# First loads of a decoder step spread over two DMA queues, and its last result row stored in halves

## The reference, cut to what matters

```python
h = rmsnorm(x, g_mix_pre)
proj = h @ w_in                      # q, k, v, the conv branch's B, C, u and two gates
...
x = x + rmsnorm(merged @ w_o, g_mix_post)
h2 = rmsnorm(x, g_ffn_pre)
...
x = x + rmsnorm(f, g_ffn_post)
x = x + jax.nn.sigmoid(x @ w_ple_gate) * (p @ w_ple)
```

## Time and profile before

| what | us |
|---|---|
| median of three runs | 2642.64 (2642.46 to 2642.98) |
| profiled execution, first to last instruction | 2641.4 |
| PE busy in it | 2631.3 |
| DVE, ACT, POOL busy | 2263.1, 1413.3, 194.9 |

### The profile page before, as it was taken

How to read it: one execution, slowest core, us unless ns; L and a number is a source line. 1 busy time by engine, 2 the same in 40 slices (tenths; PEclk the granted TensorE clock), 3 DMA queues, 4 the chain that set the end, 5 groups by cost and what they waited for, 6 DMA issues and landing times.

```text
span 2641.4 us, 55478 instructions
## 1 busy us (share of the span) xinstructions
PE 2631.3 (100%) x20853; PEld 2571.7 (97%) x20853; DVE 2263.1 (86%) x4000; ACT 1413.3 (54%) x2592; POOL 194.9 (7%) x296
## 2 busy tenths in 40 slices
PE   9999999999999999999999999999999999999999
PEld 8999999999999999999999999999999999999899
DVE  7988888888899987898888888888888768789987
ACT  6544555555566555655555555555555463445444
POOL 0221000000011000000000000000000000000000
PEclk9999999999999999999999999999999999999999
DMA  6666334333487555756566655665569575565774
GB/s 229 186 202 182 133 127 139 133 126 119 157 291 225 165 171 151 266 152 181 166 189 190 189 156 168 187 208 166 157 195 310 150 247 169 161 206 165 246 262 155
DMA packets 162481, 487.12 MB, mean 184 GB/s; under 512 B 17337, under 2 KB 51521, under 8 KB 158928
## 3 DMA queue, kind: packets, MB, share of 16 engines
q1 hardware_dynamic: 129184, 372.41, 39.9%
q0 software_dynamic: 32976, 112.38, 18.9%
q10 hardware_dynamic: 144, 0.15, 0.0%
HBM read 426.42 MB, written 57.30 MB: 183 GB/s over the span
## 4 chain that ended last, share of the span: by engine, by line
PE 65%; DVE 1%; issue 0%; ACT 0%; DVEq 0%; ACTq 0%
PE pair L1221 56%; PE pair L1186 5%; PE pair L1124 2%; PE pair L1298 1%; PE pair L1320 1%; DVE v_lo L1979 0%; DVE lo L2353 0%; PE pair L1081 0%; DVE v_lo L1976 0%; ACT o_hi L1455 0%; DVE s_raw L2278 0%; DVE s_raw L2297 0%; ACT v_hi L1390 0%; DVE lo_A L2353 0%; PE pair L1275 0%
## 5 line engine op out<-in xcount | busy, mean ns | idle before, releaser
L1221 PE MATMUL pair<-o_hi,v_hi 128*128 128x260 f32 x5840 | 1656.2, 284 | 1.9 <-DVE v_lo L1979 1.4
L1221 PE MATMUL pair<-o_hi,v_lo 128*128 128x260 f32 x5840 | 1648.9, 282 | 0.0
L1390 ACT ACTIVATE v_hi<-s_raw 128x512 fp32r<-128x512 f32 (+1 forms) x1384 | 861.7, 626 | 884.8 <-PE pair L1221 795.4
L1221 PE MATMUL pair<-lo,v_hi 128*128 128x260 f32 x4172 | 1178.5, 282 | 0.0
L1979 DVE TENSOR_TENSOR v_lo<-s_raw,v_hi 128x512 fp32r<-128x512 f32 (+1 forms) x1288 | 873.2, 680 | 296.1 <-ACT v_hi L1390 261.5
L1221 PEld LDWEIGHTS pair<-o_hi,v_hi 128*128 128x128 f32 x5840 | 1098.0, 188 | 15.6 <-issue 12.5
L1221 PEld LDWEIGHTS pair<-o_hi,v_lo 128*128 128x128 f32 x5840 | 1099.9, 188 | 0.0
L1221 PEld LDWEIGHTS pair<-lo,v_hi 128*128 128x128 f32 x4172 | 784.1, 188 | 0.2
L1390 ACT ACTIVATE v_hi<-s_one 128x512 fp32r<-128x512 f32 (+1 forms) x228 | 142.2, 626 | 192.6 <-PE pair L1221 164.2
L1221 PE MATMUL pair<-lo_E,v_hi 128*128 128x260 f32 x834 | 236.0, 283 | 0.0
L1221 PE MATMUL pair<-lo_A,v_hi 128*128 128x260 f32 x834 | 235.2, 282 | 0.0
(11 more groups left out here) (301 smaller groups left out, 2595.4 us busy)
## 6 DMA issues: line engine op xcount, KB each, us to landing
s_raw<-in_sstream SPq DMA_DIRECT2D x468, 512.0 KB, 4.9
s_one<-in_sstream POOLq DMA_DIRECT2D x168, 512.0 KB, 5.2
raw<-f_scr SPq DMA_DIRECT2D x12, 1040.0 KB, 7.7
s_raw<-in_sstream SPq DMA_DIRECT2D x32, 384.0 KB, 4.1
g_scr<-d_h SPq DMA_DIRECT2D x16, 520.0 KB, 2.7
g_in<-g_scr SPq DMA_DIRECT2D x32, 260.0 KB, 4.0
x_scr<-y_sb SPq DMA_DIRECT2D x8, 1040.0 KB, 5.3
s_one<-in_sstream POOLq DMA_DIRECT2D x32, 256.0 KB, 4.6
```

The lines of the kernel that those rows point to most:

```text
L1221: mm = pe.matmul(out, wt[:, slot, kk * P:kk * P + P], r[:, k, :], start=j in (0, 1, 3) and k == 0 and n == 0, stop=k == nk - 1 and n == 2, ...
L1390: nc.scalar.activation(v_hi[:, n % 4, 0:width], src, ACT.Copy, scale=0.5 if halved(u) else 1.0).then_inc(v_hi_rdy, 1)
```

## The change

The weight pieces of parts 0 to 2 (rows 0 to 3) leave SP's queue and go to ACT's. There they are cut otherwise: the pieces of row 0 alone count on `kv_first`, those of rows 1 to 3 on a new `kv_second`, for which PE waits ahead of row 1. The constants are split: the 16 columns of gains go first on ACT's queue (`gain_ready`), the other 280 last of its six loads; three of the six stand behind ACT's first table load and activation. ACT waits for `x_part[2]` at 16, since no weights count on it any more, and for the rest of `chan` just ahead of its first use. At the end, the upper half of row 15 is stored by itself as soon as DVE has added it (`half_out`), then row 14, then the lower half of row 15. The arithmetic is the same.

```diff
             for i, (a, b) in enumerate(X_PARTS):
                 sp.dma_start(x_raw[:, a:b, :], x_in[:, a:b, :]).then_inc(x_part[i], 16)
                 for q in (a // KH, 2 + a // KH):
-                    if i == 0:
-                        kv_piece(q, 0, 2, kv_first)
-                    elif i > 1:
+                    if i > 2:
                         kv_piece(q, a, b, s_rdy[0][q] if b % KH == 0 else x_part[i])
...
+            def last_store():
+                i = 7
+                row = d_sb[i % 2]
+                sp.wait_ge(half_out, 1)
+                sp.dma_start(y_out[2 * i + 1, :, HALF:T], row[:, 1, HALF:T]).then_inc(y_stored[i % 2], 16)
+                sp.wait_ge(x_out, 2 * i + 1)
+                sp.dma_start(y_out[2 * i, :, :], row[:, 0, :]).then_inc(y_stored[i % 2], 16)
+                sp.wait_ge(x_out, 2 * i + 2)
+                sp.dma_start(y_out[2 * i + 1, :, 0:HALF], row[:, 1, 0:HALF]).then_inc(y_stored[i % 2], 16)
...
-                gate_store(i)
+                if i < 7:
+                    gate_store(i)
+                else:
+                    last_store()
...
             for i in range(2):
-                sp.wait_ge(y_stored[i], 16 * KD // 2)
+                sp.wait_ge(y_stored[i], 16 * (KD // 2 + i))
...
                     if k == 0:
                         pe.wait_ge(kv_first, 32)
+                    if k == 1:
+                        pe.wait_ge(kv_second, 32)
...
-            act.dma_start(chan[:, :], chan_in).then_inc(chan_ready, 16)
+            act.dma_start(chan[:, 0:KD], chan_in[:, 0:KD]).then_inc(gain_ready, 16)
+            for q in (0, 2):
+                act.dma_start(s_raw[0][q][:, 0:P], sstream[0, q, :, 0:P]).then_inc(kv_first, 16)
             act.wait_ge(pool_set, 1)
             nc.scalar.activation(table_out[:, 6:7], ones[:, 0:1], ACT.Sqrt)
+            for q in (0, 2):
+                act.dma_start(s_raw[0][q][:, P:4 * P], sstream[0, q, :, P:4 * P]).then_inc(kv_second, 16)
+            act.dma_start(chan[:, KD:NCHAN], chan_in[:, KD:NCHAN]).then_inc(chan_ready, 16)
...
-            act.wait_ge(chan_ready, 16)
+            act.wait_ge(gain_ready, 16)
             for i, (a, b) in enumerate(X_PARTS):
-                act.wait_ge(x_part[i], 16 if i < 2 or b % KH == 0 else 48)
+                act.wait_ge(x_part[i], 16 if i < 3 or b % KH == 0 else 48)
...
+            act.wait_ge(chan_ready, 16)
             bias = chan[:, C_BGATE:C_BGATE + 2 * KD]
...
-                st.done(last_half(HALF, T, 2 * i + 1))
+                last_half(HALF, T, 2 * i + 1).then_inc(half_out, 1)
```

More of the change, by code:

```diff
@@ L512, in build @@
         kv_first = sem("kv_first")
+        kv_second = sem("kv_second")
+        gain_ready = sem("gain_ready")
+        half_out = sem("half_out")
         bias_half = sem("bias_half")
```

## The result

| | before | with the change |
|---|---|---|
| median of 21 runs, us | 2642.64 (2641.84 to 2644.26) | 2646.06 (2644.32 to 2648.00) |
| profiled span, us | 2641.4 | 2646.1 |
| PE busy in it, us | 2631.3 | 2631.9 |

The ratio is 1.0014, with a 95% interval of 1.0008 to 1.0019: slower by 3.4 us, where 0.6 us of gain was forecast and 2643.4 us was the upper end of the range. It is within 0.2%, as forecast, but the sign is wrong.

A forecast was written before the change was run, and what follows sets the result against it. PE was taken to bound the kernel, busy 2631.3 of 2641.4 us. Gains of 0.1 (row 0), 0.2 (row 2) and 0.3 us (end) sum to 0.6 us, from 2642.64 to 2642.0 us; range 2641.2 to 2643.4.

The forecast's parts named there:

- Start, what is added: ACT's six issues where it had one: weights for row 1 land at 7.5 us, no PE wait, 0.2 us of cover.
- a queue that is emptier: Argument that the 192 KB pieces for rows 1 to 3 on ACT's queue land at 7.1 to 8.1 us.
- Start, rows 2 and 3: x's rows 2 and 3 issued third, no weights counted: row 2 scaled by 7.8 us, PE's 0.20 us gap goes.
- a column takes twice as long at the start: PE's warm-up pace at the start: time won there may count for half, 0.06 to 0.12 us, taken as 0.1.
- the second weight pieces become the wait: Rival at row 1: pieces issued after ACT's activation land at 8.6 to 9.6 us; 2643.4 us, chance 0.15.
- The rival of issues that hold each other up: At the start, ACT's and SP's issues take twice 0.44 us, row 0 comes 1.5 us late; 2643.5 us, chance 0.05.
- a sign of being wrong: Issues of ACT or SP of 0.8 us in the first 4 us would show the prediction wrong.
- ACT's scaling of row 0: At the start, ACT's first scaling would come near 4.2 us, where it came at 4.54 us.
- the constants' rest costs nothing: The rest of the constants, issued at 2.9 us, is first used after PE's sum at 31.06 us: no cost.
- as the prediction assumed of a gain: The 0.3 us gained at the start carries through PE's sum at 31.06 us to the end.
- The end's 0.3 us: Last store of 130 KB in place of 260 KB lands 0.3 us sooner, bounds 0.1 and 0.5 us.
- the gain of 0.3 us at the start: PE's gaps ahead of rows 0 and 2 go, worth 0.1 and 0.2 us.

The follow-up runs named there:

- e3: The changed kernel, but SP holds back x's rows 2 and 3, and all behind them, until row 0's weights have landed; 2641.79 us.
- e1: The changed kernel with the new start alone; the end stores whole rows as before; 2646.11 us.
- e5: The changed kernel with 24 warm-up matmul pairs on PE in place of 9; 2644.62 us.
- e11: The changed kernel with 20 warm-up matmul pairs on PE in place of 9; 2644.64 us.
- e2: The kernel before with the new end alone, the last row stored in halves; 2641.72 us.
- e7: The changed kernel, but weights of rows 0 and 1 stay on SP's queue; only those of rows 2 and 3 go to ACT's; 2643.28 us.
- e4: The changed kernel, but SP loads x's rows 2 to 5 one at a time, in packets half as long; 2644.68 us.
- e8: The changed kernel, but ACT's first two weight pieces hold rows 0 to 3 at once and the second pair is gone; 2647.06 us.
- e10: The changed kernel, but SP waits until x's row 0 has landed before it issues x's rows 2 and 3; 2643.03 us.

## Why the prediction was wrong

*The step that failed* is "Start, what is added". It had the gains and row 0's two pieces "issued by 0.73 + 3 x 0.44 = 2.05 us", which is right (2.11), and left row 0 there: the landing of these two pieces, for which PE waits first of all, got no term in the sum and no rival. The argument given for the pieces of rows 1 to 3, that "a queue that is emptier" serves them sooner, was the wrong picture for both pairs. The old second piece took 3.5 us from issue on SP's queue, and I carried that over in effect. It took 6.7 us, because a place in one queue is no place in the other, and the change put the two-row load of x beside it at the same moment. e3 shows it by taking that load, and all behind it, away for the time of the wait: 3.3 us to landing, no gap on PE, and 4.3 us less in all.

*"Start, rows 2 and 3"* took it as safe to move x's load up from fifth to third place: "even at the old landing time" ACT would be in time. It was, in its way: row 2 was scaled from 8.14 us, earlier than 9.14 before. The load's own landing was checked; whom it pushes aside was not. Issued 1 us earlier, it landed 1 us later than before (8.1 against 7.1) and held up the weights.

*Pace had no term.* The prediction noted that a column takes twice as long at the start and used it to halve a gain. That a late row 0 could bring the lower pace back, as in the profiled change, or meet a clock that has not risen yet (e1, first entry at 13.9 us), was not weighed. In the profiled run of the change it cost 1.89 us more than before, and e5 confirms it from the other side: without the stop 24.81 us for the same instructions.

*The rival that came nearest* was "the second weight pieces become the wait". It named the pieces of rows 1 to 3 and their issue behind the activation. ACT's queue did not wait for the activation (2.20 us, not 3.5), and yet the pieces landed at 9.2 and 11.0 us, the second later than the rival's 8.6 to 9.6. PE did not wait for them, only because row 0 was later still; in e11, where row 0 came at 7.81 us, it did, for 0.68 us.

*The rival of issues that hold each other up* fell: ACT's issues took 0.40 to 0.67 us and SP's first four 1.81 / 4 = 0.45 us, side by side. SP's issue of x's rows 6 and 7, at 3.61 us, did take 1.19 us, which the prediction named as a sign of being wrong, but every load for which PE stood had been issued by then. No run shows the doubled 0.44 us from which 2643.5 us was worked out. The second issuing engine brought the issues forward, and not the landing: SP's first four loads are issued by 2.55 us, and the third lands with ACT's third at 8.1 to 8.4 us.

*What held.* ACT's scaling of row 0 moved from 4.54 to 3.88 us, and the constants' rest costs nothing. What PE's sum loses reaches the end undiminished, 4.8 us at the sum and 4.7 at the end, as the prediction assumed of a gain. The end's 0.3 us is borne out as a size in most profiles, not in the change's own: from DVE's last addition to the span's end it was 2.6 us in the two profiles with the old end (before, e1), and of the twelve with the new one 2.3 us in ten and 2.5 us in the change and in e2. The last store's time to landing shows the same: 2.0 us with the old end, 1.7 us in the ten, 2.0 us in the change and 1.9 us in e2. Why these two differ is not known, and no median tells the 0.3 us from nothing (e2).

*What stays open.* How long a stop the pace bears is not settled. For the 112 instructions e7 needed 25.09 us behind a stop of 1.28, e4 26.63 behind 1.70, e3 26.09 with none, and e8 26.18 behind 4.60: the order is not that of the stops. It is that of the time from row 0's start until the clock's record goes to 1.00: nothing in e7, where it did so at 4.9 us, 2.1 us in e3, 2.8 in e8, 3.7 in e4 and 5.7 in the change. Half of that time, since the lower granted clock is 0.50, on top of the 24.81 us of e5 gives all five within 0.3 us. What sets the moment at which the clock rises is open: with the change's start it came at 3.9 us in one profile and at 13.9 us in another (e1). And the gain of 0.3 us at the start cannot be confirmed: in e2, whose start is that of the kernel before, the sum came at 30.74 us, 0.32 earlier, so the start alone varies by as much from run to run.

## What to carry to other kernels

In the kernel before, SP's first seven loads landed in the order of their issue, 4.3 to 9.1 us. The weights moved to ACT's queue left that order: they went out beside what stood in the same place of SP's queue, 279 packets against 311 in 4 us, so that the 64 KB piece beside 520 KB, with 144 packets like it, landed at 8.4 us where the large load landed at 8.1. When you move a load, price the landing of what the next engine waits for first, and look for what now goes beside it, in both queues; if the split is wanted, hold the large load back until the small one has landed, as e3 does (4.9 us and not 8.4). A stop of PE at the start cost more than its length here: the granted clock fell to 0.50 in the 3.8 us of the profiled change, whose 112 instructions took 1.89 us more than before, and had still to rise behind the 3.20 us of e1, where they took 27.51 us.

## What the runs showed of the hardware

Equal places landing together was the surprise: 64 KB and 520 KB at 8.4 and 8.1 us, and 311 packets against 279 in the same 4 us.

The granted clock fell in a stop of 3.8 us, and stayed at 0.50 for about 6 us of work behind it. A shorter stop, 2.25 us, did it too (e10, columns as above):

```profile
10.00:12.00 2.00, 1.02 (x2) 0.72 1.02 359
12.00:14.00 2.00, 2.00 (x6) 0.50 1.04 404
14.00:16.00 2.00, 2.00 (x10) 0.93 1.04 403
```

The view of the clock needs a second look at the start. In e1, with nearly the same wait as the change (3.20 us), the stretches from 8 to 16 us read 1.00 throughout, with 4, 7, 6 and 10 instructions where the change has 4, 6, 6 and 10:

```profile
12.00:14.00 2.00, 2.00 (x6) 1.00 1.05 390
```

The instructions' own lengths tell what happened. PE of e1 in order of time, first whole, then in windows at 9.3 and 14.5 us:

```profile
8.40 27.51 PE L961 MATMUL pair<-raw,s_raw 128*128 128x260 f32 x112 [3.20 <-DMA s_raw<-in_sstream]
8.97 0.64 PE L961 MATMUL pair<-raw,s_raw 128*128 128x260 f32 x1
14.27 0.38 PE L961 MATMUL pair<-raw,s_raw 128*128 128x260 f32 x1
```

At 0.64 us an instruction ran at the lower pace, at 0.38 us at the full one. The warm-up had taken 4.21 us, at the lower pace too, so in e1 the clock did not fall in the stop: it had not risen before it. The trace's record of the clock has its first entry at 13.9 us, where the lengths change (in the profiled change at 3.9 us, within the warm-up), and where there is no entry yet the view prints 1.00. The length of an instruction, or the count in a stretch, is the surer sign.
